# An encoder layer on one core: stick-breaking attention as a backward scan over keys, and projection operands rounded from a turned input

## What is computed

```python
z = jnp.einsum('bhqd,bhkd->bhqk', qi, kf) * scale
before = kpos[None, :] < qpos[:, None]
log_beta = jax.nn.log_sigmoid(z)
log_1m = jnp.where(before, jax.nn.log_sigmoid(-z), 0.0)
tail = lax.cumsum(log_1m, axis=3, reverse=True) - log_1m
w = jnp.where(before, jnp.exp(log_beta + tail), 0.0)
```

## Time and profile before

| what | value |
|---|---|
| median of 3 runs (lowest, highest) | 1148.42 us (1148.1, 1149.21) |
| the profiled execution's own time | 1147.69 us |
| its span | 1146.0 us |
| busy: PE, DVE, ACT, POOL | 1080.7, 805.1, 574.7, 78.5 us |
| mean granted TensorE clock | 0.974 |
| transferred | 70.44 MB |
| chain that ended last: PE, DVE, ACT, issue | 81%, 8%, 6%, 2% |

### The profile page before, as it was taken

How to read it: one execution, slowest core, us unless ns; L and a number is a source line. 1 busy time by engine, 2 the same in 40 slices (tenths; PEclk the granted TensorE clock), 3 DMA queues, 4 the chain that set the end, 5 groups by cost and what they waited for, 6 DMA issues and landing times.

```text
span 1146.0 us, 12155 instructions
## 1 busy us (share of the span) xinstructions
PE 1080.7 (94%) x4844; PEld 843.8 (74%) x4844; DVE 805.1 (70%) x778; ACT 574.7 (50%) x711; POOL 78.5 (7%) x70
## 2 busy tenths in 40 slices
PE   6999999997899999979999999999999999999993
PEld 5777777886445447857888888878888878888782
DVE  2535668656454544879778686799876898867998
ACT  6313432447455551575675446743466533467353
POOL 0004113201100101410000000000000000000000
PEclk9999999978899999988999999999999999999997
DMA  7221112110000025140220401301204013026003
GB/s 223 59 65 38 37 37 74 37 38 1 1 1 1 1 85 191 74 166 1 78 69 1 147 1 37 110 1 60 88 1 147 1 37 111 1 62 232 1 1 147
DMA packets 44640, 70.44 MB, mean 61 GB/s; under 512 B 10244, under 2 KB 19752, under 8 KB 44584
## 3 DMA queue, kind: packets, MB, share of 16 engines
q1 hardware_dynamic: 43544, 69.66, 18.0%
q10 hardware_dynamic: 1040, 0.00, 0.1%
HBM read 61.27 MB, written 8.39 MB: 61 GB/s over the span
## 4 chain that ended last, share of the span: by engine, by line
PE 81%; DVE 8%; ACT 6%; issue 2%; DMA 2%; SPq 1%; DVEq 0%; POOL 0%; ACTq 0%
PE ps L677 25%; PE ps L681 24%; PE ps L679 24%; PE ps L893 2%; PE ps L753 1%; PE ps L906 1%; ACT swa_p L1206 1%; PE ps L921 1%; PE ps L861 1%; DVE out_gained L1937 1%; DVE sb_e L1724 1%; ACT sb_e L1265 1%; DMA g_pre_mix_c<-in_g_pre_mix 1%; DVE ps L1758 1%; ACT sb_w L1245 1%
## 5 line engine op out<-in xcount | busy, mean ns | idle before, releaser
L677 PE MATMUL ps<-a_op,b_op 128*128 128x512 f32 x448 | 175.7, 392 | 5.7 <-DVE b_op L1854 4.8
L677 PE MATMUL ps<-b_op,a_op 128*128 128x512 f32 x448 | 174.6, 390 | 2.7 <-issue 2.7
L679 PE MATMUL ps<-a_op,b_op 128*128 128x512 f32 x448 | 175.3, 391 | 0.0
L681 PE MATMUL ps<-a_op,b_op 128*128 128x512 f32 x448 | 175.2, 391 | 0.0
L681 PE MATMUL ps<-b_op,a_op 128*128 128x512 f32 x448 | 174.3, 389 | 0.0
L679 PE MATMUL ps<-b_op,a_op 128*128 128x512 f32 x448 | 174.3, 389 | 0.0
L677 PE MATMUL ps<-act_hi,w_hi 128*128 128x512 f32 x288 | 115.0, 399 | 3.2 <-DVE w_lo L1516 3.2
L1382 ACT CAST a_op<-f 128x1024 fp32r<-128x1024 f32 x56 | 58.8, 1049 | 116.1 <-PE ps L681 75.9
L1854 DVE TENSOR_TENSOR b_op<-wq,b_op 128x1024 fp32r<-128x1024 f32 x96 | 117.0, 1218 | 0.0
L679 PE MATMUL ps<-act_lo,w_hi 128*128 128x512 f32 x288 | 112.8, 392 | 0.0
L681 PE MATMUL ps<-act_hi,w_lo 128*128 128x512 f32 x288 | 112.6, 391 | 0.0
(11 more groups left out here) (189 smaller groups left out, 1755.8 us busy)
## 6 DMA issues: line engine op xcount, KB each, us to landing
wq<-in_w_ff_in SPq DMA_DIRECT2D x16, 1024.0 KB, 5.4
wq<-in_w_ff_out SPq DMA_DIRECT2D x16, 1024.0 KB, 5.2
stage<-in_w_in SPq DMA_DIRECT2D x18, 512.0 KB, 4.7
y<-in_x SPq DMA_DIRECT2D x4, 1024.0 KB, 9.9
stage<-in_w_out SPq DMA_DIRECT2D x8, 512.0 KB, 3.8
h_spill<-y SPq DMA_DIRECT2D x8, 512.0 KB, 2.7
h_back<-h_spill SPq DMA_DIRECT2D x2, 2048.0 KB, 11.8
out<-y SPq DMA_DIRECT2D x8, 512.0 KB, 2.7
```

The lines of the kernel that those rows point to most:

```text
L677: nc.tensor.matmul(dst, stat[0], mov[0], start=first, stop=False, skip_group_check=chained)
L679: nc.tensor.matmul(dst, stat[0], mov[1], start=False, stop=False, skip_group_check=chained)
L681: return nc.tensor.matmul(dst, stat[1], mov[0], start=False, stop=last, skip_group_check=chained)
```

## The change

1. The host passes x also in turned form (`x_turned`) and eight small vectors as one array (`columns`, 56 values a partition). TensorE's transposes of x go; ACT and DVE read the turned x from SBUF (`xt`, which lies in the place of `act_lo` and is overwritten by it). x itself is loaded after granule 1's weights and is needed only for the sums of squares; the norms are spread inside granule 1 (after f = 4) and the band matmul moves behind f = 8.
2. The recurrence's squares are rounded and summed inside granule 8 (`group_sums(0)` behind f = 34).
3. In the window stage two recurrent rows are done, and ACT, not DVE, scales the early rows. The window's probabilities are turned one bank at a time.
4. The loop has queries on partitions: 16 units u (two heads p, eight blocks t of 128 queries, t from 7 to 0), 32 heads n = 2u + a, each with 128(t+1) keys. A head is: scores for both heads of a unit, sigmoid(-z) and sigmoid(z) on ACT, an edge mask on POOL, a scan backward over the keys and one product on DVE, the turning of the weights block by block on TensorE, a copy on ACT, and the product with v. Ten recurrent rows fill it in halves; four remain behind it.
5. Of the two preload calls the one before the window stage is gone; the other stands behind granule 1's rounding.

```diff
+XT_PARTS = ((0, 0, 2), (0, 2, 4), (0, 4, 8), (1, 0, 4), (1, 4, 8))
...
+        UNITS = [(p, t) for p in range(2) for t in reversed(range(TOK))]
+        HEADS = 2 * len(UNITS)
+        CHAIN = 4
+        LEAD = 3
+        FILL_UNITS = (0, 1, 2, 3, 4, 5, 8, 9, 10, 11)
+        N_EARLY = WINDOW_ROWS + len(FILL_UNITS)
...
+            sp.dma_start(columns_c[:, :], columns).then_inc(columns_loaded, 16)
+            load_in_half(0, 0)
+            load_turned(0)
+            load_turned(1)
+            load_in_half(0, 1)
+            load_turned(2)
...
+            load_turned(3)
+            load_turned(4)
+            load_in(1, w_in[0], IN_COLS[1])
+            for i in range(4):
+                sp.dma_start(y[:, 2 * i:2 * i + 2, :], x[0, 2 * P * i:2 * P * (i + 1), :]
...
+            for u in range(len(UNITS)):
+                head_turn(2 * u)
+                if u:
+                    weighted(u - 1)
+                if u in FILL_UNITS:
+                    recurrent_out(row_of(u), range(2))
+                if u + 2 < len(UNITS):
+                    scores(u + 2)
+                head_turn(2 * u + 1)
+                if u in FILL_UNITS:
+                    recurrent_out(row_of(u), range(2, OUT_K))
...
+                nc.scalar.activation(sb_r[n % 3][:, 0:keys(n)], z, ACT.Sigmoid, scale=-1.0)\
+                    .then_inc(left_ready, 1)
+                act.wait_ge(turned_ready, win_piece(n + 1) if n < 4 else piece(n - 3))
+                nc.scalar.activation(sb_w[:, n % 4, 0:keys(n)], z, ACT.Sigmoid)\
+                    .then_inc(beta_ready, 1)
...
             act.wait_ge(v_turned, 1)
-            nc.scalar.preload_act_table_set("natural_log_exp_and_others")
...
+            for n in range(HEADS):
+                u, a = divmod(n, 2)
+                if a == 0 and u - 1 in FILL_UNITS:
+                    recurrent_row(row_of(u - 1))
+                if n + LEAD < HEADS:
+                    weights(n + LEAD)
+                turned_copies(n)
...
+                if n == RSQRT_HEAD:
                     group_rsqrt(1)
...
+                left, w = sb_r[n % 3], sb_w[:, n % 4, :]
+                dve.wait_ge(left_ready, n + 1)
+                nc.vector.tensor_tensor_scan(backward(left, 1, keys(n) - 1),
+                                             backward(left, 1, keys(n) - 1),
+                                             backward(sb_mask, S - keys(n) + 1, keys(n) - 1),
+                                             1.0, ALU.mult, ALU.max).then_inc(left_scanned, 1)
+                dve.wait_ge(left_scanned, n + 1)
+                dve.wait_ge(beta_masked, n + 1)
+                nc.vector.tensor_tensor(w[:, 0:keys(n) - 1], w[:, 0:keys(n) - 1],
+                                        left[:, 1:keys(n)], ALU.mult).then_inc(w_ready, 1)
```

More of the change, by code:

```diff
@@ L328, in slot_free @@
                 eng.wait_ge(y_ready, banks_out(g - 1 - N_IN))
[L332 to L343, removed]
-        def diagonal(s):
-            return SB[s][2] * P >= SB[s][1] * BANK
@@ new lines, in encoder_layer, with keys, pieces, win_piece @@
+        HEADS = 2 * len(UNITS)
+        CHAIN = 4
+        LEAD = 3
+        def keys(n):
+            return P * (UNITS[n // 2][1] + 1)
+        def pieces(n):
+            return -(-keys(n) // BANK)
+        def win_piece(h, c=0):
+            return 2 * h + c
+        def piece(n, c=0):
+            return 8 + sum(pieces(m) for m in range(n)) + c
+        def piece_bank(i):
+            return 4 + i % 2
+        def turned_slot(i):
+            return wt_slots[i % 3]
+        WINDOW_ROWS = 2
@@ L448, in sum_count @@
             return ahead + SUMS[s % 2].index(name) + 1
-        SPLIT_STEP = next((s for s in range(len(SB)) if early(s) >= TOK), len(SB))
         @block.sync
@@ L649, in _ @@
[L649 to L657 removed]
+            after(nc.gpsimd.memset(sb_mask[:, 0:S - P], 0.0))
+            after(nc.gpsimd.memset(sb_mask[:, S - P:S], 1.0))
@@ L1142, in _ @@
             nc.scalar.activation(lam_t[:, :], lam_t[:, :], ACT.Ln, bias=1.0).then_inc(lam_ln, 1)
-            round_inputs(0, 1, g_pre_mix_c)
+            act.wait_ge(eps_ready, 1)
+            for i in range(TOK):
+                if i % 2 == 0:
+                    act.wait_ge(x_loaded[i // 2], 16)
+                squares(i, work[:, 4, :])
+            first_rsqrt(slice(0, TOK), 0)
             spread_copy()
-            split_hi(1, 1)
             def recurrent(c):
@@ new lines, in _ @@
+            weights(2)
+            window_output(1, 1)
+            for n in range(HEADS):
+                u, a = divmod(n, 2)
+                if a == 0 and u - 1 in FILL_UNITS:
[3 more added lines that the diff above has]
+                turned_copies(n)
+                if a == 0 and u and u % CHAIN == 0:
+                    output_copy(u // CHAIN - 1)
+                if n in (3, 5):
+                    act.wait_ge(win_copied, 4)
+                    k = (n - 3) // 2
+                    nc.scalar.activation(win_sq[:, k, :], o_t[6 + k], ACT.Square)\
+                        .then_inc(grp_sq, 1)
+                if a and u in MIX_UNITS:
+                    round_group(6 + MIX_UNITS.index(u), 2 + MIX_UNITS.index(u))
+                if a and u == SPLIT_UNIT:
+                    split_hi(N_IN + 2, N_IN % 2)
+                if n == RSQRT_HEAD:
+                    group_rsqrt(1)
@@ L1773, in _ @@
-            left = list(range(early(len(SB) - 1), 2 * TOK))
+            dve.wait_ge(tables_ready, 2)
+            for n in range(HEADS):
+                u, a = divmod(n, 2)
+                stick(n)
+                if a == 0 and u - 1 in MIX_UNITS:
+                    k = MIX_UNITS.index(u - 1)
+                    rest_group(4 + k, 6 + k, act_hi, act_lo, 2 + k)
+                if a == 0 and u == SPLIT_UNIT + 1:
+                    split_lo(N_IN + 2, N_IN % 2)
+                if a and u == SUM_UNIT + 1:
+                    group_variance(1, 7)
+                if n == RSQRT_HEAD + 1:
+                    group_rsqrt(1)
@@ L1774, in _ @@
+            left = list(range(N_EARLY, 2 * TOK))
             for k in range(2):
```

846 lines of the change are left out of this document (378 added, 468 removed).

## The result

| | before | after | forecast |
|---|---|---|---|
| median, us | 1148.82 (1148.1 to 1149.37, 4 runs) | 1120.01 (1115.8 to 1121.78, 4 runs) | 1124 (1096 to 1147) |
| ratio after to before | | 0.9744, 95% interval 0.9716 to 0.9773 | |
| span of the profiled execution, us | 1146.0 | 1117.6 | 1121.5 |
| busy PE, DVE, ACT, us | 1080.7, 805.1, 574.7 | 1028.6, 804.0, 619.1 | |

What follows compares the result with a forecast made beforehand. Projection and MLP were taken as TensorE-bound, with slack at the start, window stage, loop and mixing, and DVE holding the tail. Terms -10.4 + 1.8 - 45.7 + 2.7 + 17 + 10.1 = -24.5 from 1147.69 gave 1124 us, range 1096 to 1147.

Steps and rivals of the forecast that it cites:

- term D: Behind the loop: four recurrent rows are done there, not three, +2.7 us.
- A, start: Start to granule 1's end: first projection matmul at about 8, TensorE waits about 2 for the norms, -10.4 us.
- B's +1.8: Inside granule 8: eight matmuls for the recurrence's sums, +1.8 us.
- C, window stage and loop: Window stage 42 us and loop 102, TensorE the longest engine at 92, against 189.7 before: -45.7 us.
- the two removed matrices: Old loop: the two constant matrices alone took 55 us of TensorE's time, a check on the loop's gain.
- E, loads in the mixing stage: Mixing stage: table loads for ACT's roots add 17 us, bounds 0 and 25.7.
- F, MLP: MLP: no instruction differs but for the columns' addresses, 0 us.
- G, tail: Tail: two table loads a tile make ACT's period 3.81 us and ACT the pace, +10.1 us (7 to 12).
- TensorE's clock: Rival, loop: small matmuls and transposes bring the clock down, about 1203 us if all at 1.2 GHz; chance 0.14.
- Free loads: Rival, mixing stage and tail: table loads cost nothing, 1097 us, or half of it, 1107; chance 0.13 for both.
- The round trip: Rival, loop: the ring of product, sigmoids and scores bounds it, +15 us, 1139; chance 0.14 with the slow scan.
- The slow scan: Rival, loop: scans take 3.866 us instead of 2.291, loop about 15 us longer; chance 0.14 with the round trip.

Runs made afterwards that it cites:

- the first two runs: The changed kernel with both preloads of the exp-and-ln table set, 1087.16 us; the changed kernel with one preload ahead of the last eight roots, 1109.44 us.

## Why the prediction was right, and where its sum was off

The time (1124 against 1120.0) and the side were right, and three of the four stretches by 2.2 us or less. Part of this agreement is luck, as term D shows. The mechanisms, in the order of the sum:

**A, start: -10.4 forecast; -8.2 measured with B's +1.8 taken out (-6.4 in all).** The first matmul was right (8.54). That TensorE "waits about 2 us" for the norms was not: it idles 0.1 us there, since it comes there itself only at 43. Its delay is the 8.0 us that ACT stood at the copy of the relative-position row; with the copy moved, 3.3 us came back. I had named what stood in the queue of DMAs, not what is queued behind a waiting ACT: that is the step of this term that failed. I also left out that the band's matmul (1.06) is no longer in granule 1.

**C, window stage and loop: -45.7 forecast, -52.2 measured.** The window stage took 41.3 (42 forecast), the loop 96.3 (102). The term mis-sized was the product with v, "at most 0.44 ..., of which I take 28 since that row's pair stands alone". The chain of waits of the changed kernel has

```profile
288.83 0.43 PE ps L655
...
291.47 0.81 PE ps L800 x6
...
330.16 1.51 PE ps L845 x8
...
343.18 1.68 PE ps L868 x28
```

L868 is the product for a unit of seven blocks: 1.68 / 7 = 0.24 a pair, 72 x 0.24 = 17.3 and not 28, which makes the sum for TensorE 81 rather than 92. Six transposes took 0.81 (6 x 0.136 = 0.82 by the sum), and the scores of six blocks 1.51 (1.5 x 1.08 = 1.62). Two errors offset part of that: TensorE is busy 88.3 of the loop's 96.3 us and not 81, since the first matmul of a recurrent row behind a product took 0.43 and not 0.227, and since the granted clock fell where units 6 to 8 meet (below). And the reason for the length was wrong in part: the run without rows in units 8 to 11 shows that TensorE's load there was not what set it, while in units 12 and 13 it was. The 55 us that the sum gave the two removed matrices are of the size of the gain, but no run takes them out alone.

**D, rows behind the loop: +2.7 forecast. This step failed, and its sign with it.** "Four rows behind the loop, not three" rests on a miscount. The old kernel's 13 is only a cap (`FILL_BANKS`); its table fits ten rows into the loop and leaves six behind it, as the time from the last product (427.0 and 368.3) to the first matmul of another group shows, before and after:

```profile
443.36 0.39 PE L677 MATMUL ps<-w_hi,act_hi 128*128 128x512 f32 x1
...
381.95 0.39 PE L655 MATMUL ps<-w_hi,act_hi 128*128 128x512 f32 x1
```

16.4 us are 72 matmuls of 0.227. So at the sum's own price the term was -5.4, and the forecast would have been 1116. The stretch from the last product to the first matmul whose last weights were late is 25.9 us against 25.4 all the same, because two costs came that I hadn't seen. The wait at its end is 4.9 us against 1.6, in large part for g_post_mix (2.9 with its load sooner), although the moved load was in the diff. And the first of the four rows ran at the low clock, its 12 matmuls in 5.3 us, after TensorE had idled 2.45 us for the loop's last copy, which stood behind group 1's two table loads on ACT:

```profile
368.20:373.50 5.30, 5.30 (x14) 4.13 (x13) 0.00 (x0) 4.67 (x5) 0.37 (x1) 0.50 0.73 300
```

With both preloads the same row took 2.9 us, at a granted clock of 1.00.

**E, loads in the mixing stage: +17 forecast; 21.1 come back with the preloads.** 2.8 of the 21.1 lie in D's stretch (25.9 against 23.1), nearly all of it that row at the low clock, which the sum didn't have. The mixing stage proper is 91.7 us against 73.1 with the preloads, so about 18.5, close to the forecast. In the old kernel the loads cost 19.6 in all. With the preloads the way from the loop to the last matmul is 0.8 us shorter than before: 5.4 for the two rows fewer, less 3.2 of waiting and 1.5 in the mixing stage. So the table's +20.3 against +19.7 agrees by luck: D was 8.1 too high by the count of rows, and what the sum left out made that up.

**F, MLP:** 602.2 against 602, right.

**G, tail: +10.1 forecast, +10.0 measured;** period 3.79 against 3.81. ACT is the pace, and DVE waits 1.85 us for the last root.

The rivals: **TensorE's clock** did fall in the loop, but not by what it does. The window 310 to 330, where units 6 to 8 meet and TensorE is idle a fifth of the time, is at 0.74, 281 to 310 at 1.00:

```profile
281.00:310.00 29.00, 29.00 (x218) 21.16 (x214) 18.50 (x19) 18.47 (x40) 9.62 (x11) 1.00 0.00 1
310.00:330.00 20.00, 16.11 (x82) 9.85 (x80) 12.66 (x13) 12.82 (x21) 2.33 (x6) 0.74 0.17 54
```

With twice the transposes the units around it stayed at 1.00. So the page of the Trainium skill that I weighed there (TensorE: Matmul & The Clock Gate, Part 4: PE-mode transpose), by which transposes don't bring the full clock, does not show in this loop, where they stand between other matmuls; whether a stretch of nothing but transposes would show it, no run here tells. **Free loads** fell with the first two runs. The 2.66 us a switch of the Trainium skill (ScalarE: Activation LUTs, What ACT_TABLE_LOAD costs) are not what the rows show either: 1.28 and then the activation 0.01 later. **The round trip** was there (the run without four rows), but, as I read that run and the one with twice the transposes, at about the pace of TensorE's own work and not above it: no +15. **The slow scan** was not: the rows have

```profile
L1718 DVE TENSOR_TENSOR_SCAN sb_r<-sb_r,sb_mask x32: 414/1353/2297, 262.1 to 362.6; 128x1023 f32<-128x1023 f32 x4, 128x895 f32<-128x895 f32 x4, 128x767 f32<-128x767 f32 x4, 128x639 f32<-128x639 f32 x4
```

2.297 for the longest, the uncontended 2.291 of the earlier trace rows.

## What to carry to other kernels

Count table loads when an Exp and an Ln stand side by side: preloads were worth 30 to 33 us here, about as much as the 28.8 that the whole change gained, and the cost falls where ACT's roots are a chain that others live from. When an edit moves work out of a loop or behind it, look for the wait that it filled there before pricing it by its own length, and count in the trace how much of it stood there. And when a copy waits on ACT for another engine, read what is queued behind it.

## What the runs showed of the hardware that I had not expected

The scan with a backward access pattern over 1023 keys took 2.297 us, as long as a forward one (2.291 in the earlier trace rows); no cost of the direction shows. Products of two heads with 64 output rows each and 128 moving columns went through at 0.24 us a pair in a train, against 0.44 for a single pair in the earlier trace rows. And 144 more transposes in the loop left the granted clock at 1.00, while taking four rows out of it, that is more idle time, lowered it to 0.89. The mask on POOL, 128 columns a head, took 292 ns in the median with hardly any scan on DVE, 594 with the scans and 1408 with one more DVE operation a head.
